# GpSimd's share of the conditioning row: one-input multiplications, and four k tiles in five of six late chunks

## The reference

```python
mod = (jax.nn.silu(c) @ w_ada[l] + b_ada[l])[:, None, :]
shift_m, scale_m, gate_m, shift_f, scale_f, gate_f = jnp.split(mod, N_MOD, axis=-1)
h = rms_norm(x, g_mix[l]) * (1.0 + scale_m) + shift_m
x = x + gate_m * hybrid_mixer(h, w_in[l], b_forget[l], g_out_a[l], g_out_b[l], w_out[l])
h = rms_norm(x, g_ffn[l]) * (1.0 + scale_f) + shift_f
x = x + gate_f * hierarchical_moe(h, ...)
```

## Time and profile before

| | |
|---|---|
| runs | 764.64, 768.13, 768.38 us; median 768.13 |
| span of the profiled execution, first to last instruction | 762.7 us |
| TensorE busy | 730.6 us (96%), 3883 matmuls |
| VectorE busy | 354.0 us (46%) |
| ScalarE busy | 188.0 us (25%) |
| GpSimd busy | 58.8 us (8%), 69 instructions |
| mean granted TensorE clock | 0.999 of full speed |
| DMA | 197.27 MB, 259 GB/s over the span |
| TensorE's idle time in front of `quarters`' steps, for GpSimd | 1.1 us, once |

### The profile page before, as it was taken

One profiled execution on the slowest core, in us unless ns is written; L12 is line 12 of the kernel. 1 busy time (PEld: TensorE's weight loads), 2 busy tenths in 40 slices (PEclk: granted clock), 3 DMA queues, 4 the chain that ended last, 5 costly groups with the idle time before them and its releaser, 6 DMA issues.

```text
span 762.7 us, 9761 instructions
## 1 busy us (share of the span) xinstructions
PE 730.6 (96%) x3883; PEld 485.9 (64%) x3883; DVE 354.0 (46%) x798; ACT 188.0 (25%) x412; POOL 58.8 (8%) x69
## 2 busy tenths in 40 slices
PE   6999999998889999999989999999999999999996
PEld 4677778786524434343334886788888888885442
DVE  2125666785721212121121876364276656567445
ACT  5014323533511111111011338131321111111002
POOL 3033660040000000000001000000000000000000
PEclk9999999999999999999999999999999999999999
DMA  9998956956999999999999963123454645443401
GB/s 339 339 339 249 396 192 222 354 205 261 351 377 415 416 414 416 418 413 415 419 409 368 371 227 111 46 66 111 151 181 135 197 146 185 157 175 111 165 28 58
DMA packets 78250, 197.27 MB, mean 259 GB/s; under 512 B 3343, under 2 KB 38520, under 8 KB 72312
## 3 DMA queue, kind: packets, MB, share of 16 engines
q1 hardware_dynamic: 77248, 195.37, 68.6%
q10 hardware_dynamic: 664, 0.80, 0.4%
q0 software_dynamic: 288, 0.41, 0.3%
HBM read 195.33 MB, written 1.05 MB: 257 GB/s over the span
## 4 chain that ended last, share of the span: by engine, by line
PE 75%; SPq 10%; DMA 7%; DVE 5%; ACT 1%; issue 1%; POOL 1%; DVEq 0%; ACTq 0%
PE ps L1502 18%; PE ps L1218 9%; PE ps L777 9%; PE ps L1563 9%; PE ps L1294 5%; PE ps L903 4%; PE ps L1127 4%; SPq L572 4%; PE ps L914 2%; DMA arena<-in_w_up 2%; DMA ring<-in_w_ada 2%; SPq L578 2%; PE ps L1089 2%; PE ps L1099 2%; DMA ring<-in_w_in 2%; PE ps L1303 2%
## 5 line engine op out<-in xcount | busy, mean ns | idle before, releaser
L1218 PE MATMUL ps<-ring,arena 128*64 128x512 f32 x352 | 77.6, 593 | 3.1 <-DMA ring<-in_w_up 2.5
L903 PE MATMUL ps<-hs,ring 128*128 128x256 f32 (+1 forms) x288 | 66.2, 384 | 1.0 <-DMA ring<-in_w_in 1.0
L903 PEld LDWEIGHTS ps<-hs,ring 128*128 128x128 f32 (+1 forms) x288 | 52.7, 187 | 12.7 <-issue 3.8
L1218 PEld LDWEIGHTS ps<-ring,arena 128*64 128x64 f32 x352 | 26.3, 137 | 52.5 <-issue 52.5
L2848 DVE SCALAR_TENSOR_TENSOR arena<-arena,own_rows,ps 128x256 f32<-128x256 f32 x16 | 7.7, 480 | 106.8 <-ACT arena L1884 106.8
L777 PE MATMUL ps<-hs,ring 128*128 128x256 f32 x240 | 53.3, 381 | 0.3 <-PE ps L777 0.3
L777 PEld LDWEIGHTS ps<-hs,ring 128*128 128x128 f32 x240 | 45.2, 190 | 7.1 <-issue 0.9
L1502 PE MATMUL ps<-ring,hs 128*128 128x256 f32 x176 | 41.7, 380 | 0.9 <-DVE xT L2727 0.9
L1502 PE MATMUL ps<-ring,mixT 128*128 128x256 f32 x176 | 41.7, 380 | 0.0
L1502 PE MATMUL ps<-arena,mixT 128*128 128x256 f32 x176 | 41.6, 379 | 0.0
L1294 PE MATMUL ps<-ring,arena 128*64 128x512 f32 x176 | 40.2, 598 | 1.0 <-issue 0.5
(11 more groups left out here) (483 smaller groups left out, 1215.5 us busy)
## 6 DMA issues: line engine op xcount, KB each, us to landing
ring<-in_w_down SPq DMA_DIRECT2D x23, 1024.0 KB, 18.1
ring<-in_w_gate_up SPq DMA_DIRECT2D x22, 1024.0 KB, 7.2
ring<-in_w_gate SPq DMA_DIRECT2D x18, 1024.0 KB, 17.1
ring<-in_w_up SPq DMA_DIRECT2D x18, 1024.0 KB, 17.9
ring<-in_w_ada SPq DMA_DIRECT2D x5, 3072.0 KB, 12.9
ring<-in_w_down SPq DMA_DIRECT2D x5, 2048.0 KB, 8.1
ring<-in_w_in SPq DMA_DIRECT2D x9, 1024.0 KB, 17.1
ring<-in_w_ada SPq DMA_DIRECT2D x16, 512.0 KB, 9.3
```

The lines of the kernel that those rows point to most:

```text
L903: last = pe.matmul(o[0:n, 0:L], lhsT=w[:, k, lo:lo + n], rhs=h[:, k, :], start=k == 0, stop=k == KT - 1)
L1218: last = pe.matmul(ps[WIN * h:WIN * (h + 1), 0, :].rearrange("p (g n) -> p g n", g=2), lhsT=xw[:, u, k, :], rhs=expert_gate_up(2 * n + h, ...
```

## The change

`PE_K` becomes a value for each chunk, `ADA_PE_K` = (4, 4, 5, 4, 4, 4). TensorE multiplies that many tiles, and GpSimd the rest: four in chunks 0, 1, 3, 4 and 5, three in chunk 2. GpSimd's multiplications become `tensor_scalar` with the column of `silu_c` as the scalar of each partition. They are all issued first, with no wait between them; one wait for all of them follows, then the additions onto the first tile, each behind a wait for the one before. Nothing else is moved: the places of the chunks in TensorE's list, SyncE's loads and their waits are the same.

```diff
--- before.py
+++ after.py
@@ -70,7 +70,7 @@
 ADA_HALF = D
 ADA_AT = [2048, 2816, 3584, 4352, 5120, 5376, 6144]
 ADA_N = len(ADA_AT) - 1
-PE_K = 5
+ADA_PE_K = (4, 4, 5, 4, 4, 4)
 Q = 32
 IN_WIDTH = (584, 520, 512, 512, 768)
 IN_UNITS = (5, 9, 13, 17, 23)
@@ -732,14 +732,15 @@
             for c_ in range(ADA_N):
                 w = weights("ada", c_, KT, ada_width(c_))
                 pool.wait_ge(arrived[SLOT["ada", c_]], ARRIVED["ada", c_])
-                pool.tensor_tensor(w[:, PE_K, :], w[:, PE_K, :], silu_c[:, PE_K:PE_K + 1].broadcast_to([P, ada_width(c_)]), ALU.mult).then_inc(pool_step, 1)
-                pool.wait_ge(pool_step, step.up())
-                pool.tensor_tensor(w[:, PE_K + 1, :], w[:, PE_K + 1, :], silu_c[:, PE_K + 1:PE_K + 1 + 1].broadcast_to([P, ada_width(c_)]), ALU.mult).then_inc(pool_step, 1)
-                pool.wait_ge(pool_step, step.up())
-                pool.tensor_tensor(w[:, PE_K, :], w[:, PE_K, :], w[:, PE_K + 1, :], ALU.add).then_inc(pool_step, 1)
-                pool.tensor_tensor(w[:, PE_K + 2, :], w[:, PE_K + 2, :], silu_c[:, PE_K + 2:PE_K + 2 + 1].broadcast_to([P, ada_width(c_)]), ALU.mult).then_inc(pool_step, 1)
-                pool.wait_ge(pool_step, step.up(2))
-                pool.tensor_tensor(w[:, PE_K, :], w[:, PE_K, :], w[:, PE_K + 2, :], ALU.add).then_inc(ada_pool_ready, 1)
+                first = ADA_PE_K[c_]
+                for k in range(first, KT):
+                    pool.tensor_scalar(w[:, k, :], w[:, k, :], silu_c[:, k:k + 1], None, ALU.mult).then_inc(pool_step, 1)
+                pool.wait_ge(pool_step, step.up(KT - first))
+                for k in range(first + 1, KT):
+                    if k > first + 1:
+                        pool.wait_ge(pool_step, step.up())
+                    pool.tensor_tensor(w[:, first, :], w[:, first, :], w[:, k, :], ALU.add
+                                       ).then_inc(ada_pool_ready if k == KT - 1 else pool_step, 1)
                 if c_ != 0:
                     continue
                 pool.memset(wr[:, :, GROUPS:GROUP_COLS], 0.0).then_inc(pad_ready, 1)
@@ -864,10 +865,10 @@
                 chunk_there("ada", c)
                 if c:
                     pe.wait_ge(mod_ready, c + 2)
-                for k in range(PE_K):
+                for k in range(ADA_PE_K[c]):
                     quarters(7, silu_b[:, k, :], w[:, k, :], k == 0)
                 pe.wait_ge(ada_pool_ready, c + 1)
-                quarters(7, ones[:, 0:Q], w[:, PE_K, :], last=True).then_inc(ada_rows_done, 1)
+                quarters(7, ones[:, 0:Q], w[:, ADA_PE_K[c], :], last=True).then_inc(ada_rows_done, 1)
 
             def shift_f_products(c):
 
@@ -1186,10 +1187,10 @@
                       skip_group_check=True).then_inc(rank_done, 1)
             w = weights("ada", 5, KT, ada_width(5))
             chunk_there("ada", 5)
-            for k in range(PE_K):
+            for k in range(ADA_PE_K[5]):
                 quarters(6, silu_b[:, k, :], w[:, k, :], k == 0)
             pe.wait_ge(ada_pool_ready, 6)
-            quarters(6, ones[:, 0:Q], w[:, PE_K, :], last=True).then_inc(ada_rows_done, 1)
+            quarters(6, ones[:, 0:Q], w[:, ADA_PE_K[5], :], last=True).then_inc(ada_rows_done, 1)
 
             def gather():
```

## The result

The changed kernel takes 780.05 us (median of 779.40 to 780.78) beside 768.25 us for the kernel before; the ratio is 1.0168, with a 95% interval from 1.0149 to 1.0188. The forecast was 766.5 us and its range ended at 770.3. The medians of four runs each lie 11.8 us apart; their quotient, 1.0154, isn't the ratio given for the runs but lies within its interval. The profiled execution has a span of 777.2 us, 14.5 more than before. Of 23 later runs of the kernel before, the four with a mean granted clock of 0.999 took 764.8 to 766.3 us and the five with 0.994 took 767.6 to 769.3; the profiled execution of that kernel, at 0.999, is one of the quick kind, so part of the 14.5 may be that.

A forecast was written before the change was run, and what follows sets the result against it. TensorE was taken as the bound, busy 730.6 of 762.7 us. Saved tiles and chunk 2's removed wait, less a new 0.8 us wait in chunk 1, gave -1.56 us at chunk 4: 766.5 us, range 763.0 to 770.3.

The forecast's parts named there:

- The price of the multiplication: GpSimd's one-input multiplication on 768 columns: 0.83 us, bounded by a 743 ns memset and the old 1.46 us two-input one.
- The rival "slower": GpSimd's multiplication stays at s = 1.42 because the loop costs; chunks 0 and 1 late, +1.9 us, 770.0; chance 0.13.
- Its formula: Once spacing s of GpSimd's multiplications exceeds 1.2 us, chunk 0 is late, delays the loads, and the change is 8s - 9.47 us.
- land earlier or later by as much as chunk 0's row does: Loads of chunks 1 to 4 form one full stream and shift with chunk 0's row; chunk 1 lands 0.33 us earlier.
- stand idle before 61.22 us: DMA engines are idle (share 0.06 in 55 to 60) until chunk 1's load is issued at 61.22 us.
- the sum: Chunk-by-chunk change of TensorE's last-step starts: -0.33, +0.15, -1.11, -1.44, then -1.56 us at chunk 4.
- the forecast's -1.11 us at chunk 2: Chunk 2's last step on TensorE starts at 95.19 instead of 96.30 us, without waiting for GpSimd.
- A tile is worth 0.33 us: Each 768-column k tile taken from TensorE saves 0.33 us; chunk 0's last step moves from 60.65 to 60.32.
- The tile saved in chunk 5: Chunk 5's 0.33 us on TensorE gains nothing, since TensorE waits 0.91 us behind it for VectorE's selection.
- The rival "shut out": VectorE's scaling is locked out during chunk 3's GpSimd multiplications; TensorE stands 1.6 us, time 768.1; chance 0.05.
- The rival "given back": The expert stage's full DMA stream doesn't follow TensorE; the 1.6 us becomes waits for weights, 768.1; chance 0.10.

The follow-up runs named there:

- The first experiment: Changed kernel with the old two-input multiplication put back, four tiles and no waits between multiplications: 772.14 us, ratio 1.0068.
- the experiment in chunk 1's wait: Changed kernel with six unneeded 128x512 matmuls ahead of TensorE's wait in chunk 1: chunk 4's last step at 132.23 us, against 133.87; no total time given.
- the price put right: Changed kernel with 0.0 added as a second operation of each GpSimd multiplication: 768.40 us beside 767.21 for the kernel before, ratio 1.0010.
- the last version: Changed kernel with two-operation multiplications, TensorE's tiles 4, 4, 5, 4, 2, 4, router's loads behind chunk 2: 764.80 us beside 767.24 before, ratio 0.9965.
- the two faster versions: Changed kernel, two-operation multiplications: tiles 4, 5, 5, 4, 2, 4 (764.90 us, 0.9978); tiles 4, 4, 5, 4, 2, 4 with router's loads behind chunk 2 (764.80, 0.9965).

## Why the prediction was wrong, step by step

**The price of the multiplication** is the step that failed first. The forecast took 0.83 us from the one-input rows, with 0.74 and 1.46 as ends; 2.21 us lies outside both. The error was to let the number of inputs set the bounds: the upper one assumed that the new form couldn't be dearer than the old. The row for the select showed another operation, not this form. The Trainium skill (GPSIMD Engine Reference, Engine selection) calls one-input work on GpSimd roughly line-rate. No run here shows that rate; the copy (0.82 us for 768 columns) and multiply with add (0.83 to 0.91) come near the memset (0.74), the multiplication alone doesn't. The rival "slower" had the right place and path: chunk 0 late, its loads late, chunk 1 later still. Its price was too low, and its reason, the loop, is not shown: with an added 0.0 the same multiplication is nearly as quick as a copy. Its formula with the measured spacing, (8.75 - 0.05) / 4 = 2.18, gives 8 x 2.18 - 9.47 = 8.0 us; chunk 4 shows 12.98. The first experiment has the spacing of 1.42 that the rival priced: the formula gives 1.9 us, chunk 4 shows 5.58. Two more steps make up nearly all of that difference.

**All loads "land earlier or later by as much as chunk 0's row does".** In the changed kernel chunk 0's row is 3.52 us late, and chunk 1's weights 5.57. With the router's loads behind chunk 2 in both kernels the weights are only 3.10 late (75.92 against 72.82), with a row 3.59 late (64.23 against 60.64). So 3.10 of the 5.57 go with the row, and the other 2.47 are the router's loads, which now fall on the full stream: they cost 3.85 us here and 1.38 in the kernel before. The prediction named them on GpSimd's queue and asked only when TensorE needs them, not what they take from the loads beside them. Its row for engines that "stand idle before 61.22 us" ended at 60 us. Behind that, the trace of the kernel before already shows them, first on nearly empty engines, then in a full stream:

```profile
60.00:61.00 1.00, 1.00 (x31) 0.65 (x20) 0.35 (x2) 0.00 (x0) 1.00 (x2) 1.00 0.73 47
...
66.00:67.00 1.00, 1.00 (x9) 0.91 (x7) 0.77 (x3) 0.94 (x3) 0.00 (x0) 1.00 1.08 268
```

With the router's loads late, the kernel before has a share of 0.02 in the first of these stretches and moves 421 GB/s in the second.

**The clock behind a wait.** In the sum a wait cost its own length; nowhere did it reckon with TensorE's clock. In the changed kernel, chunk 1's last step is 11.78 us late and the transposes behind it (L1015 at 101.20; as L1014 at 86.69 before) 14.51: 2.7 us of halved clock, which the experiment in chunk 1's wait gave back.

Put together, chunk 1's last step is late by 5.57 for its weights and 14.64 - 8.24 = 6.40 for GpSimd's work on them, less the margin of 0.2 that it had: 11.78. With 2.73 for the clock that is 14.51. The old wait in chunk 2 and the tiles saved in chunks 3 and 4 give back 1.5: 12.98. From there to the end the two profiled executions drift apart by 1.5 us more. Of this, 1.33 is one wait for an expert's weights (0.67 us at 359.89 before, 2.00 at 374.48 in the changed kernel); in the traces of the experiments the same wait lies anywhere between 0.32 and 1.99 us, so it is not shown that it belongs to the change. By the ratio of the runs (1.68% of 768, 12.9 us) there is no such part.

With the price put right, chunk 1's last step is 1.46 us later than forecast (84.30 against 82.84): its weights are 0.81 late instead of 0.33 early, and GpSimd takes 9.23 us instead of 8.87. With 1.7 more for the clock, the forecast's -1.11 us at chunk 2 becomes +2.07. Of the 1.14 us that the weights are off, the router's loads make 0.58: they cost 75.01 - 73.05 = 1.96 us here, by the last version, whose chunk 1 is shared out alike, and 1.38 in the kernel before. Where the other 0.56 comes from is open. So the gain that was forecast would not have come even with 0.9 us for the multiplication: chunk 4's last step is 1.61 us late, and the time is not told from no change.

**What held.** A tile is worth 0.33 us on TensorE (chunk 0 at 60.27 with the fast form, 60.32 forecast). The tile saved in chunk 5 goes into the wait behind it, which grows from 0.91 us to 1.23. In chunk 2 the wait is gone, but by luck: not because GpSimd ends sooner, but because TensorE itself comes 13 us later. The rival "shut out" is refuted: VectorE's pairs under four multiplications in a row (107.13 to 115.98) took

```profile
109.39 1.17 DVE L2257 TENSOR_SCALAR arena<-arena 128x128 f32<-128x128 f32 x2
110.66 1.07 DVE L2257 TENSOR_SCALAR arena<-arena 128x128 f32<-128x128 f32 x2
```

instead of 0.55 us: slowed, but not shut out. The first pair even lies whole inside the second multiplication (109.31 to 111.52), so for these two operations a lock held for a whole instruction is not what this trace shows. With the two-operation multiplications the pairs beside chunk 3's (96.74 to 100.33) take 1.37 and 1.00 us, and TensorE doesn't wait for them. The rival "given back" is refuted too: chunk 4 is 1.4 and 1.7 us earlier in the two faster versions, and by the ratios of 0.9978 and 0.9965 their times are 1.7 and 2.7 us lower (intervals 0.5 to 2.8 and 1.4 to 4.1), so the experts' stage doesn't swallow the gain.

## What to carry to other kernels

Bound the price of an operation that no row shows by its own form, not by a count of its inputs, and put a probe of it in an engine's idle time before building on it: a few microseconds of scratch work here would have shown 2.21 against 0.91 us. When work moves to an engine, follow everything behind it on its queue, small loads above all, and ask what those will collide with. A wait of TensorE may cost twice, once as idle time and once as a halved clock behind it, unless a later wait swallows the second part; look at the clock behind each wait, since it doesn't fall behind all of them.

## What the runs showed of the hardware

- GpSimd's `tensor_scalar` on 128x768 floats: 2.13 to 2.21 us with one operation, 0.83 to 1.08 with multiply and add or two multiplications, 2.79 with multiply and maximum. A copy takes 0.82, a multiplication by a broadcast column 1.47.
- TensorE's clock was granted at 0.50 behind waits for GpSimd of 2.13, 3.12, 3.65, 5.09, 5.84, 5.86 and 8.16 us in these chunks, and stayed at 1.00 behind those of 0.61, 1.07, 1.22, 1.23 and 1.52. The length of one wait doesn't settle it. In the routing, the same waits of 1.50 and 0.51 us for VectorE were followed by 0.50 in the kernel before with one-input multiplications and by 1.00 in the changed kernel; a wait of 2.16 us for an expert's weights left the clock at 1.00 in the kernel before, and one of 2.11 in the version with two operations was followed by 0.50.
- Five small loads (one of 16 KB, four of 32 KB) among the large ones took the stream from 412 to 166 GB/s (71 to 73 us, with and without them), and delayed 3 MB by 1.4 us in the kernel before and by 3.9 in the changed one.
